# Sparse attention layer: index scores rectified in place in PSUM, and attention by pairs of heads with short rows for the first token tile

## What is computed

```python
s = relu(einsum('bqhd,bsd->bqhs', qi, ki))
score = einsum('bqh,bqhs->bqs', wi, s)
score = where(key_pos <= q_pos, score, NEG)
_, sel = top_k(score, 64)              # 64 keys for each token
valid = sel <= q_pos
logit = einsum('bqhd,bqkd->bqhk', q, k[sel]) * 128 ** -0.5
pr = softmax(where(valid, logit, NEG))
o = einsum('bqhk,bqkd->bqhd', pr, v[sel])   # then @ w_out
```

## Time and profile before

| | us |
|---|---|
| median of 3 runs | 2652.56 |
| lowest and highest | 2649.81, 2654.16 |
| the profiled execution | 2650.54 |
| its span, first to last instruction | 2648.8 |
| TensorE busy in it | 2420.5 (91%) |
| VectorE busy | 1791.6 (68%) |
| ScalarE busy | 1350.4 (51%) |
| POOL busy | 597.4 (23%) |
| mean granted TensorE clock | 0.960 of full |

### The profile page before, as it was taken

One profiled execution on the slowest core, in us unless ns is written; L12 is line 12 of the kernel. 1 busy time (PEld: TensorE's weight loads), 2 busy tenths in 40 slices (PEclk: granted clock), 3 DMA queues, 4 the chain that ended last, 5 costly groups with the idle time before them and its releaser, 6 DMA issues. The chain is left out here.

```text
span 2648.8 us, 62481 instructions
## 1 busy us (share of the span) xinstructions
PE 2420.5 (91%) x22700; PEld 2301.2 (87%) x22700; DVE 1791.6 (68%) x4090; ACT 1350.4 (51%) x2448; POOL 597.4 (23%) x490
## 2 busy tenths in 40 slices
PE   5899787878876999999999999878999999999998
PEld 3699566467876999999999999758999999999997
DVE  6613633446655795888899666674976888998665
ACT  5632634345424566555444555535666555444554
POOL 0245134126514880000000000426850000000000
PEclk9899998989997999999999999889999999999999
DMA  9722012114202555444444455313555444444552
GB/s 300 244 96 80 17 60 88 48 53 150 90 3 89 175 184 181 165 169 158 160 167 166 174 190 179 107 47 122 187 189 165 169 163 158 160 170 162 188 184 88
DMA packets 153718, 373.93 MB, mean 141 GB/s; under 512 B 8640, under 2 KB 102736, under 8 KB 136944
## 3 DMA queue, kind: packets, MB, share of 16 engines
q1 hardware_dynamic: 151216, 369.90, 41.5%
q10 hardware_dynamic: 2368, 2.23, 0.3%
HBM read 371.05 MB, written 1.05 MB: 140 GB/s over the span
## 5 line engine op out<-in xcount | busy, mean ns | idle before, releaser
L2629 ACT ACTIVATE w_hi<-ring 128x512 fp32r<-128x512 f32 x1024 | 643.1, 632 | 683.1 <-PE bank L2684 362.8
L2635 DVE TENSOR_TENSOR w_lo<-ring,w_hi 128x512 fp32r<-128x512 f32 x864 | 594.2, 690 | 306.0 <-ACT w_hi L2629 302.3
L2666 PE MATMUL bank<-x_hi,w_hi 128*128 128x256 f32 x2048 | 578.7, 283 | 3.9 <-DVE w_lo L2635 3.7
L2684 PE MATMUL bank<-hidden_hi,w_hi 128*128 128x256 f32 x2048 | 576.7, 282 | 0.0
L2666 PE MATMUL bank<-x_hi,w_lo 128*128 128x256 f32 x2048 | 573.0, 280 | 0.0
L2666 PE MATMUL bank<-x_lo,w_hi 128*128 128x256 f32 x2048 | 571.6, 279 | 0.0
L2684 PE MATMUL bank<-hidden_hi,w_lo 128*128 128x256 f32 x2048 | 571.5, 279 | 0.0
L2684 PE MATMUL bank<-hidden_lo,w_hi 128*128 128x256 f32 x2048 | 571.0, 279 | 0.0
L361 POOL TENSOR_TENSOR w_lo<-ring,w_hi 128x512 fp32r<-128x512 f32 (+2 forms) x264 | 350.2, 1344 | 727.4 <-ACT w_hi L352 721.1
L2666 PEld LDWEIGHTS bank<-x_hi,w_hi 128*128 128x128 f32 x2048 | 385.9, 188 | 4.8 <-ACT hidden L2759 4.0
L2666 PEld LDWEIGHTS bank<-x_lo,w_hi 128*128 128x128 f32 x2048 | 386.0, 188 | 0.0
(11 more groups left out here) (518 smaller groups left out, 4226.5 us busy)
## 6 DMA issues: line engine op xcount, KB each, us to landing
ring<-in_peer_uT SPq DMA_DIRECT2D x128, 1024.0 KB, 4.9
ring<-in_peer_v SPq DMA_DIRECT2D x128, 1024.0 KB, 4.8
ring<-in_even_w_in SPq DMA_DIRECT2D x26, 1024.0 KB, 5.2
ring<-in_ada_w SPq DMA_DIRECT2D x24, 1024.0 KB, 6.4
ring<-in_odd_w_in SPq DMA_DIRECT2D x12, 1024.0 KB, 5.3
ring<-in_even_w_out SPq DMA_DIRECT2D x8, 1024.0 KB, 5.0
ring<-in_odd_w_out SPq DMA_DIRECT2D x8, 1024.0 KB, 5.2
ring<-in_peer_w_q SPq DMA_DIRECT2D x8, 1024.0 KB, 5.2
```

Source lines behind the costliest of these rows:

```text
L2629: act.activation(k.hi[q][:, :], k.ring[slot][:, q * PART:q * PART + PART], ACT.Copy).then_inc(k.hi_ready, 1)
L2635: eng.tensor_tensor(k.lo[q][:, :], k.ring[slot][:, q * PART:q * PART + PART], k.hi[q][:, :].bitcast(F32), ALU.subtract).then_inc(k.lo_read ...
L2666: mm = pe.matmul(k.bank[s][:, j * T:j * T + T], a[q][:, w], b[:, cc, :], start=(cc == 0 and n == 0), stop=(cc == KC - 1 and n == 2))
L2684: mm = pe.matmul(out, a[q][:, w], b[:, j, :], start=first and cc % 2 == 0 and n == 0, stop=last and cc % 2 == 1 and n == 2, skip_group_che ...
```

## The change

Selection. ScalarE rectifies a bank in place, in PSUM, and no longer waits for one of three buffers; TensorE's waits for a free bank count the sums (`used`) and not the rectified banks. VectorE's sums read PSUM. The sum of head 0 adds `notcausal` (0, or NEG for a key after the token), and the two mask instructions in `choose` are gone. Of the three instructions of the bias the first two become one.

Attention. A function of its own takes the place of the shared one for this layer: 8 units of two heads. A unit of token tile 0 works on keys 0 to 127 alone, one of tile 1 on all 256. Mask-add, maximum and negation are one instruction each for both heads, exponential and scaling one for each head. The product with v is one matmul for both heads and each chunk of 128 keys. The hi part of the output is now written by ScalarE, from the bank, behind its copy of `pT`; VectorE only computes the lo part, three passes after the unit's maximum. The diff, without the blocks of POOL and SP, which are as before:

```diff
--- before.py
+++ after.py
@@ -2307,7 +2307,6 @@
     def __init__(self, k, b, const, norm, work):
         self.k, self.b, self.const, self.norm = k, b, const, norm
         flat = work.rearrange("p c t -> p (c t)")
-        self.relu = flat[:, 0:6 * T].rearrange("p (n m t) -> p n m t", n=3, m=2)
         self.tmp, self.tmp_pool = flat[:, 6 * T:8 * T], flat[:, 8 * T:10 * T]
         self.best = k.sb("best8", [P, 2, 8])
         self.rotated, self.turned, self.turned_out, self.scored, self.rectified, self.used, self.q_pool, self.q_dve, self.q_turned = (
@@ -2349,15 +2348,15 @@
             self.score(pe, 3)
         if blk == 5:
             for h in range(4, I_H):
-                pe.wait_ge(self.rectified, h - 3)
+                pe.wait_ge(self.used, 2 * (h - 3))
                 self.score(pe, h)
         if blk == 6:
             pe.wait_ge(self.rotated, 8)
-            pe.wait_ge(self.rectified, 5)
+            pe.wait_ge(self.used, 10)
             self.turn(pe, self.bank(0), [b["kv"][:, m, 0:S_D] for m in range(2)])
         if blk == 8:
             for j in range(4):
-                pe.wait_ge(self.rectified, 5 + j)
+                pe.wait_ge(self.used, 2 * (5 + j))
                 if j == 0:
                     pe.wait_ge(self.turned_out, 4)
                 pe.wait_ge(*((self.q_pool, 2) if j == 0 else (self.q_dve, 2 * j + 2)))
@@ -2375,9 +2374,7 @@
 
     def rectify(self, act, h):
         act.wait_ge(self.scored, h + 1)
-        if h >= 3:
-            act.wait_ge(self.used, 2 * (h - 2))
-        act.activation(self.relu[:, h % 3, :, :], self.bank(h)[:, :].rearrange("p (m t) -> p m t", m=2), ACT.Relu).then_inc(self.rectified, 1)
+        act.activation(self.bank(h)[:, :], self.bank(h)[:, :], ACT.Relu).then_inc(self.rectified, 1)
 
     def scalar(self, act, blk):
         b = self.b
@@ -2413,22 +2410,16 @@
         for m in range(2):
             n = 2 * h + m
             dve.wait_ge(self.rectified, h + 1)
-            r, w = self.relu[:, h % 3, m, :], self.b["wi"][:, m, h:h + 1]
-            if h == 0:
-                dve.tensor_scalar(score[:, m, :], r, w, None, ALU.mult).then_inc(self.used, 1)
-            else:
+            r, w = self.bank(h)[:, m * T:m * T + T], self.b["wi"][:, m, h:h + 1]
+            if h:
                 dve.wait_ge(self.used, n - 1)
-                dve.scalar_tensor_tensor(out=score[:, m, :], in0=r, scalar=w, in1=score[:, m, :],
-                                         op0=ALU.mult, op1=ALU.add).then_inc(self.used, 1)
+            before = score[:, m, :] if h else self.const("notcausal")[:, m, :]
+            dve.scalar_tensor_tensor(out=score[:, m, :], in0=r, scalar=w, in1=before, op0=ALU.mult, op1=ALU.add).then_inc(self.used, 1)
 
     def choose(self, dve):
         S, const, best = self.k.dve, self.const, self.best
         score, bias = self.b["score"], self.b["bias"]
         dve.wait_ge(self.used, 2 * I_H)
-        S.step(dve.tensor_tensor(score[:, :, :], score[:, :, :], const("causal"), ALU.mult))
-        S.settle(dve)
-        S.step(dve.tensor_tensor(score[:, :, :], score[:, :, :], const("notcausal"), ALU.add))
-        S.settle(dve)
         for _ in range(TOPK // 8):
             for m in range(2):
                 S.step(dve.max(best[:, m, :], score[:, m, 0:P * (m + 1)]))
@@ -2437,9 +2428,7 @@
                 x = score[:, m, 0:P * (m + 1)]
                 S.step(dve.match_replace(x, best[:, m, :], x, GONE))
             S.settle(dve)
-        S.step(dve.tensor_scalar(bias[:, :, :], score[:, :, :], 10 * NEG, None, ALU.is_lt))
-        S.settle(dve)
-        S.step(dve.tensor_tensor(bias[:, :, :], bias[:, :, :], const("causal"), ALU.mult))
+        S.step(dve.scalar_tensor_tensor(out=bias[:, :, :], in0=score[:, :, :], scalar=10 * NEG, in1=const("causal"), op0=ALU.is_lt, op1=ALU.mult))
         S.settle(dve)
         S.step(dve.tensor_scalar(bias[:, :, :], bias[:, :, :], -1.0, -NEG, ALU.add, ALU.mult))
 
@@ -2476,6 +2465,126 @@
                 rotate_halves(dve, S, b["q"][:, :, j * WB:j * WB + WB], 2, const("cosA"), const("sinA"), self.tmp, self.q_dve)
 
 
+def sparse_attention(k, b, mixT):
+    nc = k.nc
+    pairs = [(m, h) for m in range(2) for h in range(0, S_H, 2)]
+    N = len(pairs)
+    scale = S_D ** -0.5
+    prob = k.sb("prob_sparse", [P, 3, 2 * T])
+    pT = k.sb("pT_sparse", [P, 2, 2 * T])
+    mx = k.sb("mx_sparse", [P, 3, 2])
+    sums = k.sb("sums_sparse", [P, 3, 2])
+    scored, maxed, exped, normed, turned, turned_out, mixed, rounded, stored = (
+        k.sem(n + "_sparse") for n in ("scored", "maxed", "exped", "normed", "turned", "turned_out", "attended", "rounded", "stored"))
+    keys = lambda u: P * (pairs[u][0] + 1)
+    scores = lambda u: k.bank[(0, 1, 6, 7)[u % 4]]
+    probs = lambda u, i: prob[:, u % 3, i * keys(u):i * keys(u) + keys(u)]
+    both = lambda x, u: x[:, 0:2 * keys(u)].rearrange("p (i t) -> p i t", i=2)
+    outs = lambda u: k.bank[4 + u % 2][:, 0:2 * P].rearrange("p (i t) -> p i t", i=2)
+    def place(u, part):
+        m, h = pairs[u]
+        return mixT[part][:, h:h + 2, m * P:m * P + P]
+    with nc.Block() as block:
+        k.begin()
+        ahead = Ahead(k)
+        @block.tensor
+        def _(pe):
+            def score(u):
+                if u >= 4:
+                    pe.wait_ge(maxed, u - 3)
+                m, h = pairs[u]
+                for i in range(2):
+                    mm = pe.matmul(scores(u)[:, i * keys(u):i * keys(u) + keys(u)], b["qT"][:, h + i, m * P:m * P + P], b["kT"][:, 0:keys(u)],
+                                   start=True, stop=True)
+                mm.then_inc(scored, 1)
+            def turn(u):
+                pe.wait_ge(normed, 2 * u + 2)
+                if u >= 2:
+                    pe.wait_ge(turned_out, u - 1)
+                for c in range(2 * keys(u) // P):
+                    mm = pe.transpose(k.bank[2 + u % 2][:, c * P:c * P + P], prob[:, u % 3, c * P:c * P + P], k.ident[:, :])
+                mm.then_inc(turned, 1)
+            def attend(u):
+                pe.wait_ge(turned_out, u + 1)
+                if u >= 2:
+                    pe.wait_ge(stored, u - 1)
+                n = keys(u) // P
+                p4 = pT[:, u % 2, 0:2 * keys(u)].rearrange("p (i c t) -> p i c t", i=2, c=n)
+                for c in range(n):
+                    mm = pe.matmul(outs(u), b["kv"][:, c, S_D:2 * S_D], p4[:, :, c, :], start=(c == 0), stop=(c == n - 1))
+                mm.then_inc(mixed, 1)
+            score(0)
+            for u in range(N + 2):
+                if u + 1 < N:
+                    score(u + 1)
+                if 1 <= u <= N:
+                    turn(u - 1)
+                if u >= 2:
+                    attend(u - 2)
+        @block.scalar
+        def _(act):
+            ahead.high(act)
+            for u in range(N + 2):
+                if u < N:
+                    act.wait_ge(maxed, u + 1)
+                    for i in range(2):
+                        act.activation(probs(u, i), probs(u, i), ACT.Exp, bias=mx[:, u % 3, i:i + 1], accum_out=sums[:, u % 3, i:i + 1]).then_inc(exped, 1)
+                if 1 <= u <= N:
+                    w = u - 1
+                    act.wait_ge(turned, w + 1)
+                    if w >= 2:
+                        act.wait_ge(mixed, w - 1)
+                    act.activation(pT[:, w % 2, 0:2 * keys(w)], k.bank[2 + w % 2][:, 0:2 * keys(w)], ACT.Copy).then_inc(turned_out, 1)
+                if u >= 2:
+                    act.wait_ge(mixed, u - 1)
+                    act.activation(place(u - 2, 0), outs(u - 2), ACT.Copy).then_inc(rounded, 1)
+        @block.vector
+        def _(dve):
+            S = k.dve
+            for u in range(N + 3):
+                if u < N:
+                    m, h = pairs[u]
+                    p2, low = both(prob[:, u % 3, :], u), mx[:, u % 3, :]
+                    dve.wait_ge(scored, u + 1)
+                    if u >= 3:
+                        dve.wait_ge(turned, u - 2)
+                    S.step(dve.scalar_tensor_tensor(out=p2, in0=both(scores(u), u), scalar=scale, in1=spread(b["bias"][:, m, 0:keys(u)], 1, 2),
+                                                    op0=ALU.mult, op1=ALU.add))
+                    S.settle(dve)
+                    S.step(dve.reduce_max(low, p2, AX_X))
+                    S.settle(dve)
+                    dve.tensor_scalar(low, low, -1.0, None, ALU.mult).then_inc(maxed, 1)
+                if 1 <= u <= N:
+                    w = u - 1
+                    dve.wait_ge(exped, 2 * w + 2)
+                    S.step(dve.reciprocal(sums[:, w % 3, :], sums[:, w % 3, :]))
+                    S.settle(dve)
+                    for i in range(2):
+                        dve.tensor_scalar(probs(w, i), probs(w, i), sums[:, w % 3, i:i + 1], None, ALU.mult).then_inc(normed, 1)
+                if u >= 3:
+                    w = u - 3
+                    dve.wait_ge(rounded, w + 1)
```

(23 more changed lines are left out.)

## The result

| | before | after |
|---|---|---|
| median, us | 2651.48 (4 runs, 2649.81 to 2654.16) | 2633.31 (4 runs, 2630.75 to 2635.57) |
| ratio to before, 95% interval | | 0.9936 (0.9923 to 0.9948), by it 17.0 us |
| span of the profiled execution | 2648.8 | 2630.3 |
| TensorE busy | 2420.5 | 2406.4 |
| VectorE busy | 1791.6 | 1774.2 |

A forecast was written before the change was run, and what follows sets the result against it. VectorE's order of work was taken to bound what could be won between 1732.5 and 1784.0 us. Selection 3.6 plus attention 10.5 gave 14.1 us, so 2650.5 became 2636.4, or 2638.5 as a median; 8-in-10 range 2631 to 2646.

The forecast's parts named there:

- The eight sums: Selection: VectorE's eight sums, reading PSUM, take about 0.43 us each, 3.5 us in all for 5.62, winning 2.1 us.
- The conflict: Selection: bias and first products of q 1 alternate with POOL's rotation of q block 0; 3.6 us won, not 6.0.
- Rival (a): Selection and attention: no conflict with POOL and a clock staying up in the drain; 17.5 us won, 2635; chance 0.12.
- The wide passes: Attention, second token tile: VectorE spends 2.58 us on each two-head pass over 256 keys.
- Rival (d): Attention: two-head mask-add and maximum run longer, say by half; 9.4 us won, 2643; chance 0.08.
- The narrow pass: Attention, first token tile: VectorE spends 1.90 us on each two-head pass over 128 keys.
- The opening: Attention's start: TensorE at 1.2 GHz binds the first passes; full clock back between 1757 and 1760 us.
- The drain: Attention's end after the last maximum: last low part at 1772.1, 1774.5 with the clock halved, 1773.0 taken.
- part 2: Attention: two-head units win 10.5 us, bounds 8.5 to 11.5.
- (b): Attention: TensorE stays at 1.2 GHz throughout, because of idle gaps of 4 us and narrow work; 2646; chance 0.12.
- (c): Out-projection: the low clock reaches on, 24.5 us of matmuls take about 18 more; 2663, slower than before; chance 0.03.
- The sum: Whole kernel: 3.6 plus 10.5 gives 14.1 us won; 2636.4 profiled, 2638.5 as a median after adding 2.0.

The follow-up runs named there:

- e3: Changed kernel with POOL's rotation of q heads 0 and 1 left out; copy of k and v to first attention scores 35.01 us, 2.30 less.
- e1: Changed selection with the attention of before; selection stretch 37.31 us, attention stretch 37.92 us, ratio to before 0.9988.
- e9: Changed kernel with the two whole-tile mask instructions back behind the sums and a plain first sum; selection 38.28 us, attention 25.96 us.
- e4: Changed kernel with POOL's rotation of q block 0 two projection blocks earlier; selection 35.00 us, attention 25.96 us, ratio to before 0.9938.
- e5: Changed kernel with the first token tile working on all 256 keys; attention 26.66 us, 1.20 more.
- e11: Changed kernel with e4 and e12 together; selection 34.54 us, attention 24.51 us, median 2632.55 us, ratio to before 0.9928.
- e12: Changed kernel with unused filler matmuls between the turns of q and 26 behind the third score; selection 36.85 us, attention 24.52 us, ratio to before 0.9940.
- after_again: Changed kernel unaltered, five more runs; median 2633.32 us, ratio to before 0.9939, selection 37.30 us, attention 25.42 us.
- e2: Selection of before with the changed attention; selection 41.27 us, attention 25.78 us, ratio to before 0.9958.
- e8: Changed kernel with ScalarE's four out-projection weight parts split behind the first pair's exponentials; attention 27.28 us, 1.82 more.
- e7: Changed kernel with unused filler matmuls between the turns of q, before attention opens; selection 36.84 us, attention 25.66 us.

## Why the prediction was right, and what was mis-sized

**Where it binds.** Right: both gains lie between the rectifying of head 4 and the out-projection, most of it on VectorE's order of work, nothing behind gives them back, and the out-projection opens with TensorE busy 24.00 of 24.00 us at full clock.

**The eight sums.** Predicted 0.43 each, so the choosing 3.5 us behind the rectifying of head 4; measured 3.23 for the eight, and the choosing after 3.27. The long instances are gone even where POOL works: its next weight parts start at 1715.99, beside the last two sums. The Trainium skill ("Perfetto Trace Analysis", Optimizing Scalar/DVE Operations) gives VectorE about 65 ns more overhead on PSUM than on SBUF; 478 for 477 ns does not show it.

**The conflict.** Predicted: the bias and the first two products of q 1 fall on POOL's rotation, 3.6 us won and not 6.0. Measured: 3.95. From the first of the eight sums to the bias it was 14.78 us (15.04 predicted) and to the rotation of q 1 20.36 (20.7). `e3` takes the conflict away and gives 2.30 more; the prediction's own difference was 2.4. Rival (a) falls in its first half by that, and with it the sum of removed instructions as an answer: `e1`, `e3`, `e9` show 3.95 for the part, 6.25 without the conflict, and 0.97 for masks of 2.87. Its second half, a clock that stays up in the drain, came true.

**The wide passes.** Predicted 2.58 us, measured 2.57: two instructions at 0.69 with their 0.03, and the two scalings at 0.62 together. Rival (d), that the two-head forms run long, falls: the maximum over two rows of 256 takes 0.69, what the earlier trace rows has for one of 512. The narrow pass was put at 1.90; VectorE took 1.58 from 1746.44 to 1748.02 while it had no low part to make.

**The opening.** The first turn was put at 5.9 us after the opening and came at 6.04. The fifth pass, the first wide one, was put at 11.2 and came at 10.37. Of these 0.8 us 0.5 is score 4, which took 1.39 us where 1.9 was charged, because the clock came back while it ran; the rest is that TensorE's turns, scores and product overlapped more than the walk had it. The clock itself was put back between 1757 and 1760, 10.9 to 13.9 us after the opening, from the stretch without a gap that it had before; it came back after 9.7, earlier than that reading allows, and in six profiles with this attention code between 9.6 and 12.0. No step of the prediction says where in this spread an execution falls: that the profile after lies at its lower end is luck. Last maximum: 20.3 predicted, 19.5 measured.

**The drain.** This is the term of the walk with the largest error. The last low part was put 26.9 us after the opening, of which 0.9 stood for a clock halved in the drain, as it was before. It ended at 24.99. The granted clock stayed at 1.00 there in the profile after, and in the later windows of `e4` and `e5` above. So the term mis-sized in part 2 is mainly the clock: 10.5 us were predicted and 12.40 measured, and of the 1.9 between them 0.8 lies in the opening, 0.9 in the drain, where the charge was made and the low clock didn't come, and 0.2 in the rest of the drain's walk. The upper bound of 11.5 was too low by 0.9 for the same reason. Rivals (b) and (c) fall with it: the clock was full from 1750.2 into the out-projection. Two numbers in them were wrong: the idle gap of TensorE that (b) puts at 4 us is 2.14 (the scores end at 1749.87 and the first turn starts at 1752.01), and the ratio of the two score rows in (c), 1.91 to 1.03, makes 24.5 us longer by 20.9 and not 18.

**The sum.** 14.1 us predicted, 16.35 measured between the marks. The forecast for the median was 2638.5, and 2633.3 was measured: inside the range of 2631 to 2646, below the forecast's own range, which began at 2635. Of these 5.2 us, 2.3 are in the sum. About 2 more are in the step from the profiled execution to the median: the text put the median 2.0 above the profiled 2650.5, from three runs; twenty-three later runs of the kernel before had their medians at 2650.3, so the profiled execution was an ordinary one and nothing was to be added. By 2650.3 less 16.4 the median would be 2633.9. The remaining 0.6 to 0.9 is within what executions differ by, as the start of the copy of k and v shows.

**What stays open.** Why the medians of `e4`, `e11` and `e12` do not show the 1.4 to 3.7 us that their marked stretches gained. `e11` has 3.7 less in the stretches and 0.8 in the median, or 2.9 by the two ratios (0.9928 and 0.9939), whose intervals overlap. A spread of 5 us in the start of the stretch, and as much behind it, can hide such a gain, but that it does is argued, not shown. The profiled run of `e11` began the stretch at 1706.59, that of after at 1703.23; that of `e4` took 866.8 us from the out-projection to the end, where after took 864.3. No version ran that is clearly faster than the change.

## What to carry to other kernels

When instructions are removed from an engine, walk the remaining ones against the other engine's timeline to see what they now fall on: here 6.0 us of removed VectorE work gave 3.95, because bias and rotation met four POOL instructions, and removing the masks gave only 0.97. An operand in PSUM takes a sum out of such a conflict at no cost in its own duration, and joining two heads in one instruction saved 0.86 of 3.90 us a pass, the cast moved to ScalarE another 0.47. And do not add a correction to a forecast that is smaller than the scatter of the runs it comes from: here 2 us, from three runs that lay 4.3 us apart, was as large an error as the whole working.

## What the runs showed of the hardware beyond that

- A tiny VectorE instruction can be held by POOL: the negation of 128x2 took 1.13 us at 1742.69, beside POOL's subtractions, and 0.17 without them, while the same operation on 128x1 took 0.153 in all sixteen units of before, two of them (1748.26, 1749.24) beside POOL's four subtractions from 1746.86 on. The Trainium skill ("SBUF — State Buffer", Who interferes with whom) counts tensor_scalar among those that can take the port pair shared with GpSimd, when its shape admits the two-port mode; the trace agrees, at two elements.

```profile
1742.69 1.13 DVE L2566 TENSOR_SCALAR mx_sparse<-mx_sparse 128x2 f32<-128x2 f32 x1
```

- The clock in a lightly loaded stretch is a matter of its own. With the same attention code it came back for good 9.7 and 9.6 (after and `after_again`), 9.8 (`e3`), 10.3 (`e2`), 11.5 (`e4`) and 12.0 us (`e9`) after the opening, and attention took 25.46 and 25.42, 25.51, 25.78, 25.96 and 25.96. The brief rise to 1.00 from 2.8 to 6.2 us after the opening, in which TensorE hardly works, is in the profile after and not in `after_again`, and changed nothing. With other attention code it was back after 6.2 (`e5`, wide matmuls) and 13.0 us (`e8`), and in `e7` it fell again after a wait of 4.44 us. Full throughout against as it came is worth 0.9 to 1.4 us of 25 here.
